# A retention stage of a diffusion block: from one head at a time to two heads side by side

## What is computed

```
qc, kc, vc = chunks of q, k, v                     # 8 heads, 64 wide for q and k, 128 wide for v
scores = einsum('bnihd,bnjhd->bnhij', qc, kc) * dmask       # dmask = exp(lag * log_g)
intra  = einsum('bnhij,bnjhe->bnihe', scores, vc)
o = retention forwards + retention of the flipped sequence, flipped back
mu, var = mean and variance of o over the 128 values of a head
o = (o - mu) * rsqrt(var + EPS) * ret_gn_g         # per head
out = (o * silu(g)) @ w_br_ret
```

## Time and profile before

| | us |
|---|---|
| median of 3 runs | 6211.31 (6208.68 to 6214.29) |
| the profiled execution | 6212.44, its span 6210.5 |
| retention C, layer 0: from its first transfer to the next stage's | 84.97 |
| retention X, layer 0 | 166.40 |
| retention X, layer 1 | 167.20 |

### The profile page before, as it was taken

The page is one execution under the profiler, slowest core; times in us unless marked ns, Lnnn a source line. Parts: engine busy times, 40 slices in busy tenths (PEclk is TensorE's granted clock), DMA queues, the critical chain, the costliest instruction groups (busy, mean ns, idle before and its releaser), DMA issues. The chain is left out here.

```text
span 6210.5 us, 70543 instructions
## 1 busy us (share of the span) xinstructions
PE 5078.8 (82%) x23958; PEld 4052.2 (65%) x23958; DVE 4306.7 (69%) x7529; ACT 1872.9 (30%) x3261; POOL 860.5 (14%) x644
## 2 busy tenths in 40 slices
PE   7697737779667677999999968979794659999998
PEld 5285626633456465998888737723573559999997
DVE  1547577748786597999999952358635977767676
ACT  0123312122112265333333311221122653333333
POOL 0000005500243000333333300000000001111110
PEclk8797868989789787999999979979897779999999
DMA  6142217711465255999999912201121347777775
GB/s 212 65 156 68 98 48 274 289 41 41 161 236 200 75 159 173 387 396 397 395 394 384 362 66 78 89 20 58 52 88 41 82 139 272 274 273 275 275 272 193
DMA packets 465786, 1173.18 MB, mean 189 GB/s; under 512 B 225468, under 2 KB 259677, under 8 KB 412575
## 3 DMA queue, kind: packets, MB, share of 16 engines
q1 hardware_dynamic: 373474, 634.44, 30.3%
q0 software_dynamic: 92160, 536.91, 22.6%
HBM read 1107.01 MB, written 64.23 MB: 189 GB/s over the span
## 5 line engine op out<-in xcount | busy, mean ns | idle before, releaser
L2145 POOL DMA_INDIRECT arena<-in_peer_uv,kept x384 | 518.9, 1351 | 3675.3 <-POOLq L2030 2038.4
L223 PE MATMUL psum<-h_hi,u_ring_hi 128*128 128x384 f32 x2048 | 694.5, 339 | 13.1 <-DVE ring_lo L2233 13.0
L223 PE MATMUL psum<-h_hi,ring_lo 128*128 128x384 f32 x2048 | 694.9, 339 | 0.0
L223 PE MATMUL psum<-h_lo,u_ring_hi 128*128 128x384 f32 x2048 | 694.0, 339 | 0.0
L223 PE MATMUL psum<-v_ring_hi,w_hi 128*128 128x512 f32 x1536 | 609.7, 397 | 6.2 <-DVE ring_lo L2238 6.2
L223 PE MATMUL psum<-ring_lo,w_hi 128*128 128x512 f32 x1536 | 604.1, 393 | 0.0
L223 PE MATMUL psum<-v_ring_hi,w_lo 128*128 128x512 f32 x1536 | 600.6, 391 | 0.0
L2238 DVE TENSOR_TENSOR ring_lo<-kept,v_ring_hi 128x1024 fp32r<-128x1024 f32 x256 | 313.8, 1226 | 300.3 <-ACT v_ring_hi L2193 295.2
L2277 DVE SCALAR_TENSOR_TENSOR arena<-arena 128x1024 f32<-128x1024 f32 x384 | 482.1, 1283 | 19.5 <-issue 0.4
L2265 DVE CUSTOM_DVE_ANT_0 arena<-arena 128x1024 f32<-128x1024 f32 x384 | 463.1, 1220 | 30.6 <-DMA arena<-in_peer_uv,kept 29.9
L2205 ACT ACTIVATE w_hi<-arena 128x384 fp32r<-128x384 f32 x256 | 134.7, 526 | 965.7 <-DVE arena L2248 965.7
(11 more groups left out here) (349 smaller groups left out, 10334.3 us busy)
## 6 DMA issues: line engine op xcount, KB each, us to landing
kept<-in_mix SPq DMA_DIRECT2D x312, 512.0 KB
kept<-in_peer_u SPq DMA_DIRECT2D x256, 512.0 KB
kept<-in_peer_uv SPq DMA_DIRECT2D x256, 512.0 KB
kept<-in_ada SPq DMA_DIRECT2D x96, 512.0 KB
gate_scratch<-arena SPq DMA_DIRECT2D x12, 4096.0 KB, 21.0
arena<-gate_scratch SPq DMA_DIRECT2D x128, 384.0 KB, 6.1
spec_scratch<-arena SPq DMA_DIRECT2D x4, 2048.0 KB, 8.5
arena<-in_k_dft_x SPq DMA_DIRECT2D x6, 1024.0 KB, 11.9
```

What stands on the lines that cost most here:

```text
L223: done = pe.matmul(out, lhs[x], rhs[y], start=first and j == 0, stop=last and j == 2)
L2145: pool.indirect_dma_start(rows[q % NBUF], None, peer_uv, bass.IndirectOffsetOnAxis(ap=row_id[q % G][:, q // G:q // G + 1], axis=0))\
```

## The change

The pair, not the head, is now the unit. Per key tile PE makes the scores of both heads, one behind the other, DVE makes both products, PE both value matmuls. Each head of a pair has two score banks of its own (`6 * h + j % 2`), two product buffers (`2 * h + j % 2`), one output bank, one mean and variance bank (`3 + c % 2`), and its own output and root buffer. There are four decay tables instead of two. The centred output and its square are written in place or into the root buffer. `stage_pair` and the `staged` semaphore are gone: the matmuls read `qk`, `v`, `ctx_k` and `ctx_v` directly. `over_heads` is gone: all eight heads are written out.

On DVE the `centre` of both heads of the pair before stand behind the second key tile, both `end` behind the fourth (in C behind the last), and the tables of the next pair are made one behind the other, with `make_exponents` of the second waiting for `complete` of the first, since both use `spare`. At the stage's start the tables of both first heads are completed before the first product.

The core of the diff:

```diff
-            def over_heads(eng, step):
-                step(0, 0)
-                step(0, 1)
-                with eng.Fori(0, 2) as i:
-                    step(2 * i, 2)
-                    step(2 * i, 3)
-                step(0, 6)
-                step(0, 7)
+            def table_of(c):
+                return (c // 2 % 2) * 2 + c % 2
+            def product(p, j, h):
+                return 2 * NJ * p + 2 * j + h + 1
...
 # scalar
+                    exponentials(0)
+                    exponentials(1)
+                    for p in range(PAIRS):
+                        if p > 0:
+                            square(2 * p - 2)
+                            square(2 * p - 1)
+                        if p < PAIRS - 1:
+                            exponentials(2 * p + 2)
+                        if p > 0:
+                            root(2 * p - 2)
+                            root(2 * p - 1)
+                        if p < PAIRS - 1:
+                            exponentials(2 * p + 3)
+                        keep(2 * p)
+                        keep(2 * p + 1)
...
 # tensor
-                        if h == 0:
-                            pe.wait_ge(staged.sem, staged.at(x + (c + 1)))
...
+                        for h in range(2):
+                            b = h * DK
+                            pe.matmul(ps[:, 6 * h + j % 2, 0:T], k[b:b + DK, jt * P:(jt + 1) * P], qk[b:b + DK, p * T:(p + 1) * T],
                                       start=True, stop=True).then_inc(pe_a.sem, 1)
...
+                    for p in range(PAIRS):
+                        scores(p, 0)
+                        scores(p, 1)
                         for j in range(NJ):
+                            values(p, j)
                             if j + 2 < NJ:
+                                scores(p, j + 2)
+                            if p > 0 and j == 0:
+                                mean(2 * p - 2)
+                                mean(2 * p - 1)
+                            if p > 0 and j == min(2, NJ - 1):
+                                variance(2 * p - 2)
+                                variance(2 * p - 1)
...
 # vector
-                    def stage_pair(x, c):
...
+                        for j in range(NJ):
+                            decayed(p, j)
+                            if p > 0 and j == 1:
+                                centre(2 * p - 2)
+                                centre(2 * p - 1)
+                            if more and j == min(2, NJ - 2):
+                                make_exponents(2 * p + 2)
+                            if p > 0 and j == 3:
+                                end(2 * p - 2)
+                                end(2 * p - 1)
+                            if more and j == min(4, NJ - 1):
+                                complete(2 * p + 2)
+                                make_exponents(2 * p + 3)
+                        if p > 0 and NJ < 4:
+                            end(2 * p - 2)
+                            end(2 * p - 1)
+                        if more:
+                            complete(2 * p + 3)
```

More of the change, by code:

```diff
@@ L952, in exponentials @@
                         last.then_inc(act_a.sem, 1)
[L954 to L970, removed]
@@ L972, in _, with square, root @@
-                    act.wait_ge(consts_in.sem, consts_in.at(32))
[L973 to L976, removed]
+                    def square(c):
+                        act.wait_ge(dve_b.sem, dve_b.at(c + 1))
+                        act.activation(root_s[c % 2], out_s[c % 2], ACT.Square).then_inc(squared.sem, 1)
+                    def root(c):
+                        act.wait_ge(var_ready.sem, var_ready.at(c + 1))
+                        act.activation(root_s[c % 2], ps[:, 3 + c % 2, 0:T], ACT.Sqrt, bias=eps).then_inc(root_ready.sem, 1)
@@ L978, in _ @@
+                    square(HEADS - 2)
+                    square(HEADS - 1)
+                    root(HEADS - 2)
+                    root(HEADS - 1)
                 @block.tensor
                 def _(pe):
[L980 to L986, removed]
@@ L988, in step, with mean @@
-                    def step(x, c):
-                        h = c % 2
-                        b = h * DK
-                        if h == 0:
-                            pe.wait_ge(staged.sem, staged.at(x + (c + 1)))
[L994 to L997, removed]
-                                      start=True, stop=True).then_inc(pe_a.sem, 1)
-                        score(0)
-                        score(1)
+                    def mean(c):
+                        pe.wait_ge(act_b.sem, act_b.at(c + 1))
+                        if c >= 2:
+                            pe.wait_ge(root_ready.sem, root_ready.at(c - 1))
+                        pe.matmul(ps[:, 3 + c % 2, 0:T], mean_h, out_s[c % 2], start=True, stop=True).then_inc(mean_ready.sem, 1)
@@ new lines, in values @@
+                    def values(p, j):
+                        kind, jt = tiles[j]
+                        x = v if kind == "own" else ctx_v
+                        for h in range(2):
+                            c = 2 * p + h
+                            pe.wait_ge(dve_c.sem, dve_c.at(product(p, j, h)))
+                            if j == 0 and p > 0:
+                                pe.wait_ge(act_b.sem, act_b.at(c - 1))
+                            last = pe.matmul(ps[:, 2 + 3 * h, 0:T], x[:, jt, c * P:(c + 1) * P], prob[:, 2 * h + j % 2, 0:T],
+                                             start=j == 0, stop=j == NJ - 1)
+                            if j == NJ - 1:
+                                last.then_inc(pe_b.sem, 1)
@@ L1062, in complete, with decayed @@
                         dve.drain()
[L1064 to L1069 removed]
+                    def decayed(p, j):
+                        kind, jt = tiles[j]
+                        for h in range(2):
+                            n = table_of(2 * p + h)
@@ new lines, in _ @@
+                    make_exponents(1)
+                    complete(1)
+                    for p in range(PAIRS):
+                        more = p < PAIRS - 1
+                        for j in range(NJ):
[16 more added lines that the diff above has]
+                            complete(2 * p + 3)
@@ L1092, in stage_retention @@
+                    centre(HEADS - 2)
+                    centre(HEADS - 1)
+                    end(HEADS - 2)
+                    end(HEADS - 1)
             consts_in.add(32)
-            for c in (act_a, act_b, root_ready, pe_b, dve_b, mean_ready, var_ready, squared, exponents, staged):
+            for c in (act_a, act_b, root_ready, pe_b, dve_a, dve_b, mean_ready, var_ready, squared, exponents):
                 c.add(HEADS)
```

140 lines of the change are left out of this document (53 added, 87 removed).

## The result

The changed kernel takes 6158.29 us (median of 5 runs, 6150.81 to 6167.65) against 6214.29 before (6208.68 to 6236.13): ratio 0.9905, 95% interval 0.9889 to 0.9921. It is faster, by 56 us.

A forecast was written before the change was run, and what follows sets the result against it. The prediction took the handing over between PE, DVE and ACT as the bound, no engine being full. Gains of 13.0 in C and 2.0 and 4.0 in the X stages, 19 us, gave 6192; range 6165 to 6207.

The forecast's parts named there:

- as summed: Stages C and both X, scores one after another: 13.0 + 2.0 + 4.0 = 19 us off, 6192; chance 0.45.
- the two heads' scores overlap: Rival in the X stages: a score beside the other head's costs 0.43 more; 21 off, 6171; chance 0.38.
- middle pair: Stage X, each of two middle pairs: 35.8 us against 35.0 before, 0.8 lost each, 2.0 in all with the clock.
- first pair: Stage X, pair without ends, bounded by PE: 23 us (21 to 26) against 35.2 before, 12 gained.
- The sign that the text named for an overlap: Stage X: distance between the pairs' first scores 33 if the scores overlap, 35 to 37 if serial.
- first product: Start of stage X: first product at 12.5 us against 10.9 before, 1.6 lost, as the second table comes too.
- last pair with tail: End of stage X: 50.3 us against 43.8 before, 6.5 lost; bounds 48 to 52.
- idle time beneath two ends: Stage X, middle pair: PE stands idle some 7 us ahead of the fifth key tile's values.
- eight changes of rows: Stage X, middle pair, first score to first variance: 19 matmuls with 8 changes between 64 and 128 rows, 18.1 us.
- C: Stage C, bounded by DVE: 66.7 us against 79.7 before, 13.0 gained; bounds 9 and 16.
- The clock rival: Rival in X: PE's clock falls beneath the ends and stays; 19 us a middle pair, 6249 at three of six; chance 0.07.
- The rival that X gives back: Rival: X middle pairs 2 us longer each than forecast, 8 to 12 us lost over X, 6203; chance 0.10.

The follow-up runs named there:

- e1: The changed kernel with both heads' scores reading the first head's keys and queries, rows 0 to 63, so serial: 6193.23 us, 0.9967 to the kernel before.
- e8: The changed kernel with PE taking value and score of one head, then of the other, behind the first two tiles: 6219.31 us, 1.0002 to the kernel before.
- e4: The kernel before with heads written out and operands read where they lie, without the copies, heads one after the other: 6169.33 us, 0.9932.
- e7: The changed kernel with the same instructions in another order on DVE, ACT and PE: 6110.38 us, 0.9831 to the kernel before.
- e3: The kernel before with its eight heads written out, no register loop, copies kept: 6212.72 us, 0.9994.

## Why the prediction was wrong

**The step that failed** is the choice between the forecast "as summed", with scores one after another (0.45), and the rival "the two heads' scores overlap" (0.38). The rival happened. In the terms of the sum, the step is the 0.86 us that it charges for each of the second head's scores (19 matmuls at 0.86 in a middle pair, 20 in the first pair): they cost nothing. With serial scores (e1) the three stages are 36.6 us longer than in the changed kernel, and the forecast was 38.1 too long for them; of the 36.6, some 8 are the clock in one first pair. What spoke for the rival stood in the text: own banks and disjoint rows. What spoke against it was that no such neighbours had been measured, and that each matmul is two instructions with weights of their own. The sign that the text named for an overlap came too: the pairs' first scores are 32.6 and 31.8 apart, for its 33. By the Trainium skill, TensorE: Matmul & The Clock Gate, Part 3 (Packing small matmuls — row/col tiling), different row groups run concurrently. By that rule the rival was the result, and the trace agrees: 1.06 us for two scores.

**The rival was mis-sized too**, which is why even its 6171 is 13 too high. I priced the second score at one half of a matmul, 0.43, on the idea that only its first pass of two could hide. It costs nothing, so 0.86 is saved each time: 5 times in a middle pair, 4.3 us and not 2.6 (the text had three halves at the pair's start, where two whole ones are saved); 4 times in the first pair. With that term alone the same sum gives 157.8 - 3.4 - 3 x 4.3 = 141.5 for X, where 140.6 were measured. From 2.6 to 4.3 in six later pairs and from 2.6 to 3.4 in two first pairs are 12 of the 13 us.

**The other steps of X**, read in e1, where scores are serial as in the sum (layer 0, layer 1; forecast): first product 12.4, 12.7 (12.5); first pair 21.1, 29.3 (23); middle pairs 35.4, 35.3, 35.3, 35.8 (36); last pair with tail 49.6, 48.8 (50.3); in all 153.8, 161.9 (157.8). The first pair was bounded by 21 to 26, and its clock went beyond that once. In the changed kernel with overlap: 12.4, 19.4, 32.6, 31.8, 44.5. The idle time beneath two ends was 8.4 for 7. The sum of a middle pair counts eight changes of rows up to the variance where the order has seven, 0.2 too much.

**C**: 15.0 gained for 13.0, within the bounds; first product 8.0 (7.8), pairs as above, last 21.0 for 23.1, of which the overlap is 1.4 by e1.

**The clock rival** did not come: PE did fall to 1.2 GHz behind each pause of 8 us (3.78 for two value matmuls), and was back within the next group. But e8 shows that PE can stay at 1.2 GHz for 32 us while busy, with single values and scores in turn. The text's remark that values now come in twos leaned the right way but isn't the whole answer: in e1, also in twos, PE stayed low for 20 us once. **The rival that X gives back** did not come, in time or in mechanism: it wanted middle pairs of 38, and they took 35.3 to 35.8 in e1. X does give something back, but only against e4, 0.8 to 2.2 a stage in spite of the overlap.

**What I never costed** is the copies by themselves. The sum replaced whole pairs by whole pairs, so it came out right without them, but its story of a middle pair was wrong: that it goes from 35.0 to 35.8 because little changes. A middle pair of X in layer 0 takes 35.0 before, 33.8 without the loop, 29.6 without the copies, then 35.4 with the heads paired and serial, 32.6 and 31.8 with the overlap, and 25.1 in the order of e7. Two large terms had cancelled.

## What to carry to other kernels

Matmuls that use 64 rows of the array belong side by side in the queue, on different rows and with banks of their own: the second is then free, and with a matmul of 128 rows between them it costs its full time again. (That they need banks of their own was not tested.) Before an elaborate pairing, remove what makes PE pause: 2 us of copies cost 4.2 a pair, since the clock mostly fell behind them. And when two or more independent items share a queue, lay out the short dependent steps of the one between the long steps of the other; the same instructions in another order were worth 43 us in the stages here, where the whole change was worth 57.

## What the runs showed of the hardware that I had not expected

- A float32 score of 64 rows and 512 columns beside one on the other 64 rows: 1.06 us for both with the change of rows, 0.86 without it; one alone costs 0.86. The overlap is whole in spite of the two passes of each. The Trainium skill, TensorEngine Tiling (Array Packing), Overview (Theoretical Speedup), gives up to 2 times for a dimension of at most 64. The traces agree: four scores take 3.63 us in e1 and 1.92 in the changed kernel with one change of rows each, that is 2 times without that change.
- The clock fell to 1.2 GHz in the second matmul behind a pause of 2.0 us and stayed there for some 7 us (e3, 1354 to 1361). In e4, where PE pauses 1.14 us a head at most, it stayed at 2.4 GHz head after head. In the kernel before a pause of 2.12 us passed without a fall and one of 1.81 did not, so the length of the pause alone doesn't settle it.
- At 1.2 GHz PE stayed for 32 us while busy throughout, with single values and scores in turn (e8). With two and two it rose 3 to 6 us after the first value in the four X stages of the changed kernel and its repeat; in e1, two and two but serial, after 3 us in layer 0 and after 20 in layer 1. So the alternation alone doesn't settle it, and what does is left open.
